# Two half transfers for each weight piece, and down products by steps over both columns

## The reference

```
hid = silu(einsum('nd,edf->nef', x, wg)) * einsum('nd,edf->nef', x, wu)
y = einsum('nef,efd->nd', hid * combine[..., None], wd)
```

## Time and profile before

| | |
|---|---|
| runs (us) | 1924.73, 1918.86, 1927.50; median 1924.73 |
| the profiled execution (us) | 1917.56, its span 1915.7 |
| mean granted clock of TensorE | 0.968 of full speed |
| busy: PE, DVE, ACT | 1786.6, 478.2, 384.2 us |
| DMA | 609.47 MB, mean 318 GB/s |

### The profile page before, as it was taken

The page is one execution under the profiler, slowest core; times in us unless marked ns, Lnnn a source line. Parts: engine busy times, 40 slices in busy tenths (PEclk is TensorE's granted clock), DMA queues, the critical chain, the costliest instruction groups (busy, mean ns, idle before and its releaser), DMA issues.

```text
span 1915.7 us, 21714 instructions
## 1 busy us (share of the span) xinstructions
PE 1786.6 (93%) x8848; PEld 1052.3 (55%) x8848; DVE 478.2 (25%) x1238; ACT 384.2 (20%) x759; POOL 40.7 (2%) x52
## 2 busy tenths in 40 slices
PE   4999999989998979999999997999988999999986
PEld 2678544346635858744435565854434778444443
DVE  0243411015200341411112434231101343211102
ACT  1232200013102660210002222210001343000002
POOL 1000000000000000000000000000000000000000
PEclk9999899999999989999999998999999999999989
DMA  9988799996997335499998884579999547899970
GB/s 324 364 289 356 277 427 427 427 411 245 356 357 254 107 119 189 167 412 427 427 428 332 305 315 192 198 288 427 427 428 410 182 188 290 351 426 426 427 302 22
DMA packets 134022, 609.47 MB, mean 318 GB/s; under 512 B 12485, under 2 KB 19277, under 8 KB 108960
## 3 DMA queue, kind: packets, MB, share of 16 engines
q1 hardware_dynamic: 116880, 589.32, 77.4%
q10 hardware_dynamic: 12528, 10.70, 1.8%
q0 software_dynamic: 4512, 8.02, 1.1%
HBM read 606.15 MB, written 8.92 MB: 321 GB/s over the span
## 4 chain that ended last, share of the span: by engine, by line
PE 77%; DMA 15%; DVE 3%; ACT 3%; issue 2%; ACTq 1%; DVEq 0%; SPq 0%; POOLq 0%
PE PS L934 22%; PE PS L1476 18%; PE PS L1487 9%; DMA arena<-in_moe_wu 7%; PE PS L1440 6%; DMA arena<-in_moe_wg 6%; PE PS L964 4%; PE PS L1016 3%; PE PS L984 2%; PE PS L1420 1%; DMA arena<-token_rows,IDX 1%; PE PS L1453 1%; DMA ring<-in_w_mod 1%; PE PS L1002 1%; DVE RS L1614 1%
## 5 line engine op out<-in xcount | busy, mean ns | idle before, releaser
L1476 PE MATMUL PS<-ring,arena 128*64 128x512 f32 x1312 | 393.4, 605 | 14.3 <-DMA arena<-in_moe_wu 7.6
L1476 PEld LDWEIGHTS PS<-ring,arena 128*64 128x64 f32 x1312 | 125.1, 140 | 208.0 <-issue 208.0
L865 ACT ACTIVATE arena<-PS 128x512 f32<-128x512 f32 (+2 forms) x131 | 71.4, 545 | 829.3 <-PE PS L1467 334.0
L1988 DVE TENSOR_TENSOR arena<-arena,PS 128x512 f32<-128x512 f32 x32 | 33.5, 1046 | 588.6 <-PE PS L1476 588.6
L934 PE MATMUL PS<-HS,ring 128*128 128x256 f32 x768 | 173.7, 384 | 4.7 <-ACT arena L725 3.0
L1476 PE MATMUL PS<-arena 128*64 128x512 f32 x576 | 170.9, 597 | 1.8 <-DMA arena<-in_moe_wg 1.8
L934 PEld LDWEIGHTS PS<-HS,ring 128*128 128x128 f32 x768 | 144.6, 191 | 31.4 <-issue 9.2
L1440 PE MATMUL PS<-arena 128*128 128x256 f32 (+3 forms) x688 | 145.2, 367 | 10.2 <-ACT arena L865 4.3
L1487 PE MATMUL PS<-ring,arena 128*64 128x512 f32 x656 | 148.8, 595 | 0.5 <-DVE arena L1969 0.5
L934 PE MATMUL PS<-arena,ring 128*128 128x256 f32 (+1 forms) x672 | 145.6, 377 | 2.3 <-ACT arena L655 1.1
L1440 PEld LDWEIGHTS PS<-arena 128*128 128x128 f32 (+1 forms) x688 | 119.0, 197 | 51.3 <-issue 22.7
(11 more groups left out here) (327 smaller groups left out, 1689.9 us busy)
## 6 DMA issues: line engine op xcount, KB each, us to landing
ring<-in_w_mod SPq DMA_DIRECT2D x48, 2048.0 KB, 13.3
ring<-in_moe_wu SPq DMA_DIRECT2D x41, 2048.0 KB, 18.7
ring<-in_moe_wd SPq DMA_DIRECT2D x41, 2048.0 KB, 23.5
ring<-in_moe_wg SPq DMA_DIRECT2D x41, 2048.0 KB, 24.4
arena<-in_moe_wg SPq DMA_DIRECT2D x24, 2048.0 KB, 20.9
HS<-in_moe_wu SPq DMA_DIRECT2D x12, 2048.0 KB, 18.9
arena<-in_moe_wu SPq DMA_DIRECT2D x12, 2048.0 KB, 22.2
arena<-in_moe_wd SPq DMA_DIRECT2D x12, 2048.0 KB, 27.5
```

What stands on the lines that cost most here:

```text
L865: A(dst, src, func).then_inc(S(sem), 1)
L1476: ins = mm(PS[64 * e:64 * e + 64, b, :], XG[:, k, 64 * e:64 * e + 64], w[:, k], start=(k == 0), stop=(k == KD - 1))
L1988: tt(by_k(HID), row(SG), row(bank(here[1])), ALU.mult).then_inc(S("hid"), 1)
```

## The change

Each piece is moved by two transfers. Each takes half of the middle index of the place: k = 0 to 3 and 4 to 7 for wg and wu and the mixers' pieces (8 KB in each partition), f = 0, 1 and 2, 3 for wd. Before each half SyncE waits for `used(..., half)`. For expert pieces the count is now that of the half: "up" is raised twice in each projection, after k = 3 and after k = 7; "down" is raised three times in each pair. For all other pieces both halves wait for the same count as before. `landed` waits for both halves. The down products now run f = 0, 1 for both output columns, then f = 2, 3 for both; the wait for "wts" stands before the second of the four blocks. The other engines' counts follow.

```diff
-            pe.wait_ge(S(f"landed{SLOT[n]}"), 16 * LOADS[n])
+            pe.wait_ge(S(f"landed{SLOT[n]}"), 32 * LOADS[n])
...
-                    "wg": lambda: ("up", 2 * (NPAIR * l + c % NPAIR) + 1),
-                    "wu": lambda: ("up", 2 * (NPAIR * l + c % NPAIR) + 2),
-                    "wd": lambda: ("down", 2 * (NPAIR * l + c % NPAIR) + 2)}[kind]()
+                    "wg": lambda: ("up", 4 * pair + 1 + half),
+                    "wu": lambda: ("up", 4 * pair + 3 + half),
+                    "wd": lambda: ("down", 3 * pair + 1 + 2 * half)}[kind]()
...
-                if BEHIND[n] is not None:
-                    wait(sp, *used(BEHIND[n]))
-                sp.dma_start(slot_view(kind, SLOT[n]), src_of(kind, l, c)).then_inc(S(f"landed{SLOT[n]}"), 16)
+                dst, src = slot_view(kind, SLOT[n]), src_of(kind, l, c)
+                h = dst.shape[1] // 2
+                for half in range(2):
+                    if BEHIND[n] is not None:
+                        wait(sp, *used(BEHIND[n], half))
+                    sp.dma_start(dst[:, h * half:h * half + h], src[:, h * half:h * half + h]).then_inc(S(f"landed{SLOT[n]}"), 16)
...
-                    act.wait_ge(S("up"), 2 * n + 1)
+                    act.wait_ge(S("up"), 4 * n + 2)
...
-                        act.wait_ge(S("down"), 2 * n + j + 1)
+                        act.wait_ge(S("down"), 3 * n + j + 2)
...
-                    ins.then_inc(S(sem), 1)
+                        if len(ws) == 2 and k == KD // 2 - 1 or k == KD - 1:
+                            ins.then_inc(S(sem), 1)
...
-                def down(ws, j, b):
-                    for f in range(4):
+                def down(ws, j, b, fs=range(4)):
+                    for f in fs:
...
-                    down(ws, 0, here[0]).then_inc(S("down"), 1)
+                    down(ws, 0, here[0], (0, 1))
                     if more:
                         pe.wait_ge(S("wts"), n + 2)
-                    down(ws, 1, here[1]).then_inc(S("down"), 1)
+                    down(ws, 1, here[1], (0, 1)).then_inc(S("down"), 1)
+                    down(ws, 0, here[0], (2, 3)).then_inc(S("down"), 1)
+                    down(ws, 1, here[1], (2, 3)).then_inc(S("down"), 1)
...
-                    v.wait_ge(S("up"), 2 * n + 2)
+                    v.wait_ge(S("up"), 4 * n + 4)
```

More of the change, by code:

```diff
@@ L395, in slot_view, with used @@
             return v.rearrange("p (k n) -> p k n", k=8)
-        def used(n):
+        def used(n, half=1):
             kind, l, c = CHUNKS[n]
             a = l // 3
+            pair = NPAIR * l + c % NPAIR if kind in ("wg", "wu", "wd") else None
             return {"mod": lambda: ("mod_rows", 12 * l + c + 1),
```

## The result

| | before | changed |
|---|---|---|
| median of 20 runs (us) | 1922.67 (1915.98 to 1930.32) | 1928.35 (1922.58 to 1934.01) |
| ratio to before | | 1.0031, 95% interval 1.0019 to 1.0044 |
| the profiled execution's span (us) | 1915.7 | 1924.2 |

The change costs 0.31%, +5.7 us by the medians (by the ratio's interval 3.7 to 8.5 us). That is a real loss, smaller than the 0.5% that I took as the bound of "no change". The three runs behind the forecast had their median at 1924.73; over 20 runs of the same kernel it is 1922.67.

What follows compares the result with a forecast made beforehand. The prediction took expert stages to be bound by the transfer stream: 4 x (2.7 us strips - 2.2 us early half) = +2.0 us on the 1924.73 us median, so 1926.7 us; own range 1919 to 1934, 8-in-10 range 1912 to 1945.

Steps and rivals of the forecast that it cites:

- What bounds the stage: Expert stages: bound by the stream of transfers; six pieces of a pair need 29.5 us, TensorE 25.9 us.
- The early half: Start of each expert stage: 1 MB issued at half a projection fills idle stream, gaining 2.2 us a layer, 8.8 in all.
- From the third release on the queue doesn't empty in either kernel.: Later in each expert stage: transfers stay queued, so no idle stream time is gained or lost there.
- Strips: Expert stream, 37 pieces a layer: 128 more strips cost 0.073 us a piece, 2.7 us a layer, 10.8 us in all.
- The dear and the free strips: Rivals on 8 KB strips: dear, 0.2 us a piece, 1945.5 us, chance 0.12; free, no cost, 1915.4 us, chance 0.20.
- Twice as many transfers: SyncE's issue and the queue: doubled transfers cost 0, at most 0.02 us a piece; an issue takes 0.33 to 0.43 us.
- the gap between transfers: Rival, expert streams: engines stand still between transfers; 3.0 us at 0.02 us each, +74 us at 0.5 us; chance 0.01.
- the rival after the Trainium skill's fixed cost: Expert streams: about 2 us in line per transfer would add some 296 us; of the gap kind, whose chance is 0.01.
- Down by steps, waits for wts and ys: TensorE's down products: still 16 products and 7.02 us a pair; reordering, bank changes and waits cost 0.
- The early half brings nothing: Rival, start of expert stages: something takes the 2.46 us back, leaving the strips' +10.8 us, 1935.5 us; chance 0.08.
- The clock: Rival, last up products: half clock in three more layers, +4.6 us, 1931.3 us; inside the forecast, jointly 0.59.

Runs made afterwards that it cites:

- e1: Changed kernel, but both halves of an expert piece wait until the whole place has been used; 1936.82 us, ratio 1.0068 to the kernel before.
- e4: Kernel before with only each layer's tenth and twelfth piece in halves, each waiting for its half place; down products whole; 1920.81 us, ratio 0.9988.
- e5: Kernel before with every expert piece from the tenth in four transfers (4 KB strips), all waiting for the whole place; 1962.09 us, ratio 1.0195.
- e6: Changed kernel with halves only for each layer's tenth to fifteenth piece, all others whole; 1916.08 us, ratio 0.9954 to the kernel before.
- e7: Kernel before with expert pieces from the tenth in two transfers of gapped 4 KB strips, waiting for the whole place; 1963.08 us, ratio 1.0214.
- v2: Kernel before with each layer's tenth to fifteenth piece in quarters, issued in turn, and down products by four steps; 1912.36 us, ratio 0.9940.
- e3: Kernel before with only the down products taken by steps over both columns, transfers whole; 1922.81 us, ratio 0.9995.
- v1: Kernel before with each layer's tenth to thirteenth piece in quarters, issued in turn, each waiting for its quarter place; 1919.72 us, ratio 0.9976.
- e2: Kernel before with every piece in two transfers, partitions 0 to 63 and 64 to 127, strips unchanged; 2900.55 us, ratio 1.507.

## Why the prediction was right

Time, range and sign held; I forecast +2.0 us, and +5.7 us came. That 1926.7 us lies only 1.7 us from the measured 1928.35 is partly luck: the median that I added to was 2.1 us too high, and the difference that I added 3.7 us too small.

- **What bounds the stage.** Right. e1, e4, e5, e6, e7 and v2 change only transfers and waits for places (v2 and e6 the order of the down products too, which costs nothing by e3), and the idle time plus the strips' price gives six of the eight changes at one clock within 4 us (the far ones are e1, 5.9 us, and v2, 4.5 us).
- **The early half, 2.2 us a layer.** Right in mechanism, and near in size. SyncE issued it at 207.86 where I had 207.4. The four stages stand 12.2 us less in the first pair of profiles and 11.4 us less in the second, 3.0 us a layer, but idle time isn't the whole account: in the window from 207 to 211 the changed kernel's engines move 160 GB/s at share 0.49, which is 327 GB/s for the time they are busy (318, 328 and 334 in layers 1 to 3), where a queued stream moves 421 / 1.01. So a transfer that met an idle queue kept the engines busy for longer than its bytes need; why, no run shows. 1 MB at 327 GB/s is 3.2 us of busy time for 2.46 us of stream. With this 0.7 us a layer taken off, the early half is worth 2.3 us a layer, the sums of the table rise by up to 3 us, and those of the changed kernel, e4 and v1 meet the times at one clock within 1 us. That of e6, which had met it without this term, is then 3 us off, so the term is not settled.
- **"From the third release on the queue doesn't empty in either kernel."** True of both, but for a reason that I did not give. e4 and v1 show that a stream that starts earlier does run dry at the down release unless that is split as well. In the changed kernel the split of wd and the down products by steps do this. I had costed the steps at nothing and also credited them with nothing; without them a part of the gain is lost (e4 against e6: -4.3 and -10.1 us at one clock; from 22 to 40 us into a stage the engines stand for 1.3 us a layer in e4 and for 0.2 us in e6 and in the changed kernel).
- **Strips, 0.073 us a piece, 2.7 us a layer.** Right: 421 GB/s, as forecast, and e5 and e7 confirm the straight line. The dear and the free strips, which had 0.32 of the chances, are both out.
- **Twice as many transfers: 0.** Right by e5 and e7, whose rates agree with four and with two transfers a piece. One premise was wrong: SyncE's issue isn't always 0.33 to 0.43 us. In a full queue it took 2.13 us a half (last section), which still stayed under the 2.46 us that 1 MB needs. By this the gap between transfers, and with it the rival after the Trainium skill's fixed cost ("DMA: Bandwidth & Descriptors", on the anatomy of one DMA), is out for a stream that is queued. The Trainium skill's figure there is measured on transfers issued by GpSimd, and these are SyncE's.
- **Down by steps, waits for wts and ys: 0.** Right (e3, 7.02 us). The change adds three increments a pair (two on "up", one on "down"), not the four that I counted; they had been put at nothing either way.
- **The early half brings nothing.** Out: e1 is slower than the changed kernel, by 8.5 us in the medians and 5.8 us at one clock.
- **The clock.** I looked for it in the last up products and put it at up to 4.6 us. It lay elsewhere too, and moves single executions by more. Against the 29 runs of the kernel before, with a mean clock of 0.9633, the changed kernel's 20 have 0.9616 and a mean time that is 4.2 us longer; by the line 2.3 us of this go with the clock, and 1.9 us are left, near the forecast of +2.0. The +5.7 us are against the 20 runs measured beside it, whose clocks aren't on record, so how much of them goes with the clock isn't shown. Whether the changed kernel itself lowers the clock stays open: kernels with longer waits for transfers (e1, e5, e7) have lower clocks, but so have e4 and v1, whose waits are shorter. The mLSTM's stage alone differed by 7.5 us between the first two profiles, and by 3.2 us the other way between the second two.

## What to carry to other kernels

When a stage is bound by a stream that waits for places, count the time in which the DMA engines stand, place by place, through all releases of the first turn: making the first release early can move a part of the idle time to a later one, unless that release is split too. In this kernel splitting paid only for the few pieces that met an idle queue; every later piece paid for its shorter strips. A difference of a few microseconds between two profiles must first be compared in stages that the change doesn't touch, and with the granted clock of many runs.

## What the hardware showed beside this

**Half of the partitions, half of the rate.** In e2 the engines' share is 1.01 at 229 GB/s: they are busy all the time and move half as much. Two transfers in one queue, for partitions 0 to 63 and 64 to 127, did not add up. The Trainium skill, "SBUF — State Buffer", says in its section on the DMA port swizzle that partitions 0 to 63 reach only 8 of the 16 ports, some 218 GB/s, and in the section after it on issuing two DMAs for both halves that they serialize, with a gain of 6% over one. The trace agrees, with 229 GB/s from 300 to 350 us and 212 to 221 GB/s in three other full windows.

**SyncE can be held up by its own queue.** Late in an expert stage the changed kernel's issues take far longer than 0.33 us. The changed kernel, around the wg and wu pieces of layer 0's last pair, then the kernel before at the same pieces:

```profile
363.64 6.30 SPq L468 DMA_DIRECT2D ring<-in_moe_wg  x1
369.99 4.32 SPq L468 DMA_DIRECT2D ring<-in_moe_wu  x2
```

```profile
365.54 0.33 SPq L464 DMA_DIRECT2D ring<-in_moe_wg  x1
365.91 0.43 SPq L464 DMA_DIRECT2D ring<-in_moe_wu  x1
```

The changed kernel issues a half each 2.2 us (2.13 us of issue) and has some 27 us of transfers, about 11 halves, outstanding; the kernel before had up to 32 us outstanding, 6 or 7 pieces, with issues of 0.43 us. So what fills up is not bytes but something that grows with strips or transfers. The kernel before shows it too, where its pieces have strips of 2 KB: at the start of the program the fifth to the tenth issue each hold SyncE for 5.2 us or more; the fifth is this one.

```profile
21.83 5.21 SPq L464 DMA_DIRECT2D ring<-in_attn_w_qkv  x1
```

It cost nothing here: the changed kernel's chain does run along SyncE's issues from 350 to 376 us, but from 340 to 404 us the DMA engines keep a share of 1.01 or 1.02, and the piece issued at 376.53 stands in the queue for 27.00 us more. A SyncE that also served another queue or a short wait would have been late by as much.
